# Low-rank products of a two-block model: row groups in turn, latents on more rows, two thin projections in one slab

## What is computed

```python
wl, al, gl = 64, 64 and 160 columns of ps
log_w = -softplus(-(w0 + tanh(wl) @ w_up)) - 0.5     # decay: rank 64
a = sigmoid(a0 + al @ a_up)                          # rate:  rank 64
g = sigmoid(gl) @ g_up                               # gate:  rank 160 = 128 + 32
if vl is not None:                                   # layer 1 only
    v = v + (v_first - v) * sigmoid(v0 + vl @ v_up)  # value: rank 32
...
y = group_norm(wkv7_scan(...)) * lnx_g + lnx_b
y = (y + bonus) * g
mixed = br_gate[0] * (y @ proj_a) + br_gate[1] * (pooled @ proj_b)
```

## Time and profile before

| | before |
|---|---|
| median of 3 runs | 2925.84 us (2925.13 to 2927.65) |
| profiled execution, first to last instruction (span) | 2918.1 us |
| TensorE matmul busy | 2791.1 us, 96% of the span |
| VectorE busy | 1587.6 us, 54% |
| ScalarE busy | 988.9 us, 34% |
| GpSimd busy | 200.0 us, 7% |
| mean granted TensorE clock | 0.976 of full speed |

### The profile page before, as it was taken

How to read it: one execution, slowest core, us unless ns; L and a number is a source line. 1 busy time by engine, 2 the same in 40 slices (tenths; PEclk the granted TensorE clock), 3 DMA queues, 4 the chain that set the end, 5 groups by cost and what they waited for, 6 DMA issues and landing times.

```text
span 2918.1 us, 46007 instructions
## 1 busy us (share of the span) xinstructions
PE 2791.1 (96%) x19577; PEld 2317.3 (79%) x19577; DVE 1587.6 (54%) x2309; ACT 988.9 (34%) x1354; POOL 200.0 (7%) x251
## 2 busy tenths in 40 slices
PE   8899999999999999998899999999988999999998
PEld 7778888897788888777878788887667778888887
DVE  5658777854677777465443553334575443543334
ACT  5643222335532212333333332223533333332223
POOL 4100000000000000010040000000020030000000
PEclk9999999999999999799999999999889999999999
DMA  4334555421145554210022322322220013223222
GB/s 150 101 104 131 180 165 173 156 64 53 52 130 177 176 168 152 66 58 12 3 77 89 99 90 98 101 97 72 72 64 6 24 52 101 95 93 101 95 93 72
DMA packets 238532, 281.98 MB, mean 97 GB/s; under 512 B 7444, under 2 KB 224856, under 8 KB 238344
## 3 DMA queue, kind: packets, MB, share of 16 engines
q1 hardware_dynamic: 225312, 227.07, 24.3%
q0 software_dynamic: 12896, 52.11, 6.0%
q10 hardware_dynamic: 136, 0.03, 0.0%
HBM read 277.09 MB, written 2.10 MB: 96 GB/s over the span
## 4 chain that ended last, share of the span: by engine, by line
PE 91%; DVE 4%; ACT 3%; issue 2%; DMA 0%; ACTq 0%; DVEq 0%; POOL 0%; POOLq 0%
PE psum L2386 25%; PE psum L2388 25%; PE psum L2387 25%; PE psum L2445 1%; PE psum L2446 1%; PE psum L2447 1%; PE psum L2887 1%; PE psum L2902 1%; DVE wlo L1522 1%; PE psum L2484 1%; PE psum L2870 1%; PE psum L2797 1%; ACT whi L848 1%; PE psum L2821 1%; PE psum L2835 1%
## 5 line engine op out<-in xcount | busy, mean ns | idle before, releaser
L2386 PE MATMUL psum<-hh,whi 128*128 128x512 f32 (+1 forms) x2040 | 794.4, 389 | 19.5 <-DVE hl L1562 6.6
L1522 DVE TENSOR_TENSOR wlo<-raw,whi 128x2048 fp32r<-128x2048 f32 x222 | 517.3, 2330 | 514.7 <-ACT whi L848 514.1
L2387 PE MATMUL psum<-hl,whi 128*128 128x512 f32 (+1 forms) x2040 | 787.6, 386 | 0.0
L2388 PE MATMUL psum<-hh,wlo 128*128 128x512 f32 (+1 forms) x2040 | 786.9, 386 | 0.0
L848 ACT ACTIVATE whi<-raw 128x2048 fp32r<-128x2048 f32 x222 | 423.8, 1909 | 550.7 <-PE psum L2388 550.7
L2386 PE MATMUL psum<-mh,whi 128*128 128x512 f32 (+1 forms) x1248 | 486.3, 390 | 3.1 <-issue 2.3
L2387 PE MATMUL psum<-ml,whi 128*128 128x512 f32 (+1 forms) x1248 | 480.1, 385 | 0.0
L2388 PE MATMUL psum<-mh,wlo 128*128 128x512 f32 (+1 forms) x1248 | 479.8, 384 | 0.0
L2386 PEld LDWEIGHTS psum<-hh,whi 128*128 128x128 f32 x2040 | 388.1, 190 | 104.0 <-issue 25.2
L2388 PEld LDWEIGHTS psum<-hh,wlo 128*128 128x128 f32 x2040 | 387.8, 190 | 76.9
L2387 PEld LDWEIGHTS psum<-hl,whi 128*128 128x128 f32 x2040 | 388.0, 190 | 75.9 <-issue 1.0
(11 more groups left out here) (451 smaller groups left out, 2848.0 us busy)
## 6 DMA issues: line engine op xcount, KB each, us to landing
rest<-in_ada_w POOLq DMA_DIRECT2D x64, 768.0 KB, 5.3
raw<-in_w_gu SPq DMA_DIRECT2D x44, 1024.0 KB, 5.1
raw<-in_w_in SPq DMA_DIRECT2D x34, 1024.0 KB, 5.2
raw<-in_w_mlp_in SPq DMA_DIRECT2D x32, 1024.0 KB, 5.4
raw<-in_w_mlp_out SPq DMA_DIRECT2D x32, 1024.0 KB, 5.1
raw<-in_w_out SPq DMA_DIRECT2D x16, 1024.0 KB, 5.1
raw<-in_w_down SPq DMA_DIRECT2D x16, 1024.0 KB, 5.1
raw<-in_w_mem_kv SPq DMA_DIRECT2D x8, 1024.0 KB, 5.2
```

What stands on the lines that cost most here:

```text
L1522: ins = dve.tensor_tensor(wlo[:, g % 2, :, :], raw[:, g % 2, :, :], f32(whi[:, g % 2, :, :]), ALU.subtract)
L2386: pe.matmul(out, whi_, xhi, start=first, stop=False)
L2387: pe.matmul(out, whi_, xlo, start=False, stop=False)
L2388: return pe.matmul(out, wlo_, xhi, start=False, stop=last)
```

## The change

- **Decay beside rate.** `lw` and `la` are issued in turn, tile by tile, instead of four and four.
- **Gate latents on more rows.** The 32 weight columns of `gl1` are copied side by side into the 128 columns of the slab while ScalarE and VectorE make `whi` and `wlo` (`latent_parts`, a broadcast read). The job so writes the 32 latents four times, on rows 0, 32, 64 and 96. In layer 0 each of the four gate tiles takes its own copy (`gate_rows`). The slab's load is 32 columns wide instead of 128.
- **Layer 1: both in one slab.** `v_down` is loaded beside the 32 gate columns, and the 64 columns are copied twice: gate latents on rows 0 and 64, value latents on rows 32 and 96 (`value_rows`). Slab and job `vl` are gone. `lv` takes rows 32 and 96 in turn, the gate's last 32 latents rows 0 and 64 in turn.
- **Gate order.** All four 128-row gate matmuls, then the four 32-row ones, then `gr`; no gate tile is left between `gr` and `g1`.
- **Loads.** `v_up` and the last 32 rows of `g_up` are loaded in four pieces each on GpSimd's queue (one before), and five more small rows of shift coefficients are loaded at the program's start on SyncE's queue.

```diff
+def gate_rows(l, t):
+    a = 64 * (t % 2) if l else 32 * t
+    return slice(a, a + 32)
+def value_rows(t):
+    a = 64 * (t % 2) + 32
+    return slice(a, a + 32)
...
             self.lin("gl1", l, 1, 1)
-            if l:
-                self.lin("vl", l, 1, 1)
             self.slab_jobs("k2", l, 0, 2)
...
+        def latent_parts(dst, src, g):
+            n = 64 if latents[g] else 32
+            x = src[:, g % 2, :, 0:n].rearrange("p k (a b) -> p k a b", a=1).to_broadcast([P, KT, P // n, n])
+            return dst[:, g % 2, :, 0:P].rearrange("p k (a b) -> p k a b", b=n), x
...
-                slab(plan.slab["gl1", l, 0], cols(w)[:, :, 14 * P:15 * P], n=P)
+                slab(plan.slab["gl1", l, 0], cols(w)[:, :, 14 * P:14 * P + 32], n=32)
                 if l:
-                    slab(plan.slab["vl", l, 0], cols(d["v_down_2"][0]), n=32)
+                    sp.dma_start(raw[:, plan.slab["gl1", l, 0] % 2, :, 32:64], cols(d["v_down_2"][0])).then_inc(s_vdown, 16)
...
-                act.activation(GL[0:32, 1, :], GL[0:32, 1, :], ACT.Sigmoid).then_inc(S("gate_latent"), 1)
+                for a in (slice(0, 32), slice(64, 96)) if l else (slice(0, P),):
+                    ins = act.activation(GL[a, 1, :], GL[a, 1, :], ACT.Sigmoid)
+                ins.then_inc(S("gate_latent"), 1)
...
                 for t in range(4):
                     p = start("lw", l, t)
                     done(pe.matmul(p, WA[0:HD, t * P:(t + 1) * P], LA[0:HD, :], start=True, stop=True))
-                for t in range(4):
                     p = start("la", l, t)
                     done(pe.matmul(p, WA[HD:P, t * P:(t + 1) * P], LA[HD:P, :], start=True, stop=True))
-                if l:
-                    evacuated(pe, J["vl", l, 0, 0])
-                    for t in range(4):
-                        p = start("lv", l, t)
-                        done(pe.matmul(p, VU[0:32, t * P:(t + 1) * P], VL[0:32, :], start=True, stop=True))
+                for t in range(4) if l else ():
+                    a = value_rows(t)
+                    p = start("lv", l, t)
+                    done(pe.matmul(p, VU[a, t * P:(t + 1) * P], GL[a, 1, :], start=True, stop=True))
...
-                gate(0)
-                gate(1)
+                p = [start("g", l, t) for t in range(4)]
+                for t in range(4):
+                    pe.matmul(p[t], GU[:, 0, t * P:(t + 1) * P], GL[:, 0, :], start=True, stop=False)
+                for t in range(4):
+                    a = gate_rows(l, t)
+                    done(pe.matmul(p[t], GU[a, 1, t * P:(t + 1) * P], GL[a, 1, :], start=False, stop=True))
                 pe.wait_ge(S("gn_inv"), l + 1)
                 for t in range(4):
                     done(head_factors(start("gr", l, t), t))
-                gate(2)
-                gate(3)
```

More of the change, by code:

```diff
@@ L579, in x_ready @@
                 evacuated(eng, J["fd", ((ver - 6) // 2, len(CHUNKS2) - 1), t // 2, t % 2])
+        latents = {plan.slab["gl1", l, 0]: l for l in range(2)}
+        def latent_parts(dst, src, g):
+            n = 64 if latents[g] else 32
+            x = src[:, g % 2, :, 0:n].rearrange("p k (a b) -> p k a b", a=1).to_broadcast([P, KT, P // n, n])
+            return dst[:, g % 2, :, 0:P].rearrange("p k (a b) -> p k a b", b=n), x
         def bc(m, n=4):
@@ L812, in _ @@
                 pool.dma_start(WA[HD:P, :], d["a_up_2"][l]).then_inc(s_lora, 16)
-                if l:
-                    pool.dma_start(VU[0:32, :], d["v_up_2"][0]).then_inc(s_lora, 16)
+                for t in range(4) if l else ():
+                    s = slice(t * P, (t + 1) * P)
+                    pool.dma_start(VU[value_rows(t), s], d["v_up_2"][0, :, s]).then_inc(s_lora, 16)
                 pool.wait_ge(S("decays"), 3 * l + 3)
@@ L826, in _ @@
                 pool.dma_start(GU[:, 0, :], d["g_up_2"][l, 0:P, :]).then_inc(s_lora, 16)
-                pool.dma_start(GU[0:32, 1, :], d["g_up_2"][l, P:P + 32, :]).then_inc(s_lora, 16)
+                for t in range(4):
+                    s = slice(t * P, (t + 1) * P)
+                    pool.dma_start(GU[gate_rows(l, t), 1, s], d["g_up_2"][l, P:P + 32, s]).then_inc(s_lora, 16)
                 pool.dma_start(PW, d["pool_w_2"][l].rearrange("g c d -> c g d")).then_inc(s_lora, 16)
@@ L1233, in _ @@
                 hi(plan.slab["gl1", l, 0] + 1)
[L1234 to L1237, removed]
+                own_part("gl1", 0, 0, c0 + 14, GL[:, 1, :])
                 evacuated(act, J["gl1", l, 0, 0])
@@ L1520, in lo @@
                     ins = dve.tensor_tensor(wlo_wide, raw_wide, f32(whi_wide), ALU.subtract)
+                elif g in latents:
+                    if latents[g]:
+                        dve.wait_ge(s_vdown, 16)
+                    low, x = latent_parts(wlo, raw, g)
+                    ins = dve.tensor_tensor(low, x, f32(latent_parts(whi, raw, g)[0]), ALU.subtract)
                 else:
@@ L2020, in _ @@
                 lo(plan.slab["gl1", l, 0] + 1)
[L2021 to L2024, removed]
+                before_part("gl1", 0, 0, V("mu_shift_2", m0 + 14), GL[:, 1, :])
                 for s in range(2):
@@ L2762, in _ @@
                 linear("gl1", l, 0, h, blocks=1)
[L2763 to L2764 removed]
                 linear("k2", l, 0, h)
[L2767 removed]
+                small = 128 * l + (32 if l == 0 else 96)
                 pe.wait_ge(s_lora, small)
@@ L3086, in _ @@
                 pe.wait_ge(S("gate_latent"), 2 * l + 2)
[L3087 to L3093, removed]
-                gate(0)
-                gate(1)
+                pe.wait_ge(s_lora, small + 96)
+                p = [start("g", l, t) for t in range(4)]
+                for t in range(4):
+                    pe.matmul(p[t], GU[:, 0, t * P:(t + 1) * P], GL[:, 0, :], start=True, stop=False)
+                for t in range(4):
+                    a = gate_rows(l, t)
+                    done(pe.matmul(p[t], GU[a, 1, t * P:(t + 1) * P], GL[a, 1, :], start=False, stop=True))
                 pe.wait_ge(S("gn_inv"), l + 1)
```

42 lines of the change are left out of this document (24 added, 18 removed), and 2 rows, old and new, of the table tiles.

## The result

The changed kernel takes **2957.32 us** (median of 4 runs, 2955.59 to 2961.43), beside 2925.49 for the kernel before in the same measurement: a ratio of 1.0108, with a 95% interval of 1.0094 to 1.0123. It is 1.1% slower; 2904 was forecast, and "slower" had a chance of 0.02.

A forecast was written before the change was run, and what follows sets the result against it. TensorE was taken as the bound, 91% of the chain that ended last; gains of 22.05 us off a 2918.1 us span gave 2896.05, plus 7.7 to the median, so 2904 us, range 2900.5 to 2912.5 with the low-clock rival.

The forecast's parts named there:

- 22.05 us off a span of 2918.1: Whole kernel: gains 1.7 + 5.44 + 4.75 + 1.66 + 5.1 + 3.4 us, leaving a span of 2896.05.
- Edits at no cost: Splits, larger sigmoid, start-up issues and extra GpSimd pieces: all hidden in slack; 0.6, 1.6 or about 0.5 us each if not.
- a pause at each alternation: Rival, chance 0.03: switching row groups costs 0.3 us each time instead of overlapping; loss of 5.6 us, time 2931.4.
- Low-rank stage, layer 0: `lw` and `la` alternated on two row groups take 3.75 us instead of 5.45: gain 1.7, bounds zero to 1.8.
- the assumed offset of 0.1: Layer 0's low-rank stage: the two row groups start 0.1 us apart; gain 1.8 if this vanishes.
- Layer 1: Low-rank stage: job `vl` gone, 5.44 us; `lw`, `la`, `lv` in 5.9 instead of 10.65, 4.75; full clock behind, 1.66.
- the clock's term: Layer 1's slab behind `lv`: full clock instead of half, gain 1.66 us, zero if the clock falls all the same.
- Gate stages: Layer 0 in 12.8 us instead of 17.95, gain 5.1; layer 1 in 13.5 instead of 16.93, gain 3.4.
- the wait that was forecast as 2.0 us: Before `g1`, both layers: TensorE waits 2.0 us for VectorE to free gate tile 0's bank, a new wait.
- That 5.6: Gate stages: eight 128-row instructions start at half clock, full clock returning midway; 5.6 us, bounds 5.0 and 6.9.
- The weighed estimate of 1.12 us: Layer 0's 32-row gate part on four row groups: 8 x 0.43 / 3.07 = 1.12 us, by the skill's speedup.
- The second rival: Chance 0.1: the clock falls in `gr` and the new wait, `g1` starts at half clock; 1.7 us per layer, time 2908.

The follow-up runs named there:

- after_pad112: The changed kernel with the filler tile `padding` back at 112 words instead of 113: 2906.18 us, ratio 0.9943 to the kernel before.
- gap256: The kernel before with 64 words put between `whi` and `wlo` and taken off the padding, moving `wlo` by 256 bytes: 2923.26 us, ratio 1.0007.
- both64: The kernel before with 16 filler words ahead of the slabs, so weights and activations all lie 64 bytes higher: 2924.17 us beside 2920.8.
- pad112_again: The changed kernel with `padding` at 112 words, measured a second time: 2903.29 us, ratio 0.9947 to the kernel before.
- gates_old: The changed kernel with padding at 112 and the gate order of the kernel before, keeping latents on more rows: 2913.15 us, ratio 0.9969.
- before_pad113: The kernel before with `padding` at 113 words instead of 112 and nothing else: 2971.72 us, ratio 1.0166.
- gap32: The kernel before with 8 words put between `whi` and `wlo` and taken off the padding, moving `wlo` by 32 bytes: 2972.84 us, ratio 1.0179.
- after_pad96: The changed kernel with `padding` at 96 words: 2955.34 us, ratio 1.0115 to the kernel before.
- before_pad48: The kernel before with a smaller padding, all activations 256 bytes lower: 2920.53 us beside a median of 2918.28.

## Why the prediction was wrong

**The step that failed** is the sum itself, "22.05 us off a span of 2918.1". It takes all that isn't listed as unchanged, and so sets the cost of the padding line to nothing; the part "Edits at no cost" doesn't name it. That line sets the pace of some 9,300 matmuls, and at 48.7 us it costs twice the sum of all gains. No rival had it: the one on the slow side was a pause at each alternation, and these pauses aren't there. With the pace restored the time was near the forecast, 2906.18 and 2903.29 for 2904. In part that is luck: the kernel before was faster in those two measurements as well (2923.03 and 2920.20, where the forecast started from 2925.84), and the gain was 16.9 us both times, not 22. The terms of the sum, against `after_pad112`:

**Low-rank stage, layer 0** (gain 1.7 predicted). The two row groups start within 0.01 us of each other, eight times:

```profile
1234.71 0.69 PE L2801 MATMUL psum<-rest 64*128 64x512 f32 x1
1234.72 0.69 PE L2803 MATMUL psum<-rest 64*128 64x512 f32 x1
1235.25 0.59 PE L2801 MATMUL psum<-rest 64*128 64x512 f32 x1
...
1238.35 0.50 PE L2417 MATMUL psum<-hh,whi 128*128 128x512 f32 x1
```

3.64 us for 5.45: gain 1.8, the assumed offset of 0.1 isn't there.

**Layer 1** (5.44 + 4.75 + 1.66). TensorE's order and ScalarE's evacuations there:

```profile
2077.37 0.69 PE L2801 MATMUL psum<-rest 64*128 64x512 f32 x1
...
2081.01 2.45 PE L2807 MATMUL psum<-rest 32*128 32x512 f32 x8
2083.38 0.50 PE L2417 MATMUL psum<-hh,whi 128*128 128x512 f32 x1
```

```profile
2066.60 0.69 ACT L1247 ACTIVATE rest<-psum,omm 128x512 f32<-128x512 f32 x1 [2.95 <-PE psum L2419]
...
2077.48 0.69 ACT L1247 ACTIVATE rest<-psum,omm 128x512 f32<-128x512 f32 x1 [2.62 <-PE psum L2419]
...
2089.16 0.69 ACT L1247 ACTIVATE rest<-psum,omm 128x512 f32<-128x512 f32 x1 [2.25 <-PE psum L2419]
```

`gl1` and the second job of `k2` stand 10.88 us apart, two jobs of 5.44: `vl` is gone and no wait has come for it. The small products take 6.01 us (5.9 predicted), and the slab behind them 5.78 to its first evacuation, where it took 7.48: the clock is full there, as forecast. Gains 5.44, 4.64 and 1.70.

The last two are too large as gains of the change, since they are taken from one trace of before, in which the clock happens to fall within `lv`. In two of the other three traces of that program at the same pace, `gap256` and `both64`, it doesn't, and the small products take 9.08 us instead of 10.65. `gap256`:

```profile
2089.90 2.41 PE L2772 MATMUL psum<-rest 64*128 64x512 f32 x5
...
2095.35 3.69 PE L2780 MATMUL psum<-rest 32*128 32x512 f32 x8
2098.98 0.50 PE L2386 MATMUL psum<-hh,whi 128*128 128x512 f32 x1
```

There the gain is 3.07, and a half-clock spell of the same 6.8 us comes later (2123.9 to 2130.7 for 2091.9 to 2098.8). From the first `lw` of layer 1 to its first gate product the four traces of before's program take 262.1 to 263.3 us, mean 262.7; the four of the changed one at that pace take 257.6 to 261.5, mean 259.8. So 2.9 us are won where 4.75 + 1.66 = 6.4 were forecast: the clock's term, and 1.6 us of the one before it, priced a spell whose place changes from one execution or copy to the next.

**Gate stages** (12.8 and 13.5 us predicted, 12.06 and 13.91 measured). Layer 1's, and the wait that was forecast as 2.0 us:

```profile
2337.11 6.12 PE L3117 MATMUL psum<-rest 128*128 128x512 f32 x8
2343.16 1.99 PE L3120 MATMUL psum<-rest 32*128 32x512 f32 x8
2345.08 3.71 PE L2824 MATMUL psum<-ident,hn 128*64 128x128 f32 x64
2351.02 0.47 PE L2417 MATMUL psum<-hh,whi 128*128 128x512 f32 x1 [2.23 <-DVE rest L2273]
```

It is 1.97 us in layer 0 and 2.23 here, released by VectorE's multiplication by `g`. The eight full-row instructions took 5.31 and 6.05 us against 5.6 forecast, the small ones 1.07 on four row groups (1.1) and 1.92 on two (1.8). That 5.6 was met is in part luck as well: the forecast has them begin at half clock, but in layer 0 the clock was full when they began and fell later, and in layer 0 of `pad112_again` and in both layers of the changed kernel's own trace all eight ran at full clock, in 3.61 us. The wait ahead of `g1` was 3.12, 2.85 and 2.10 us there. The weighed estimate of 1.12 us for the four-group part rests on the 3.07 times that the Trainium skill gives (TensorE: Matmul & The Clock Gate, Measured speedup vs the span model); the 1.07 here, 8 x 0.43 / 1.07 = 3.2 times, agrees with it.

**The second rival** (chance 0.1: the clock falls once more at `gr` and the wait) came true in part, beside the forecast: in layer 1 the clock is at its half from 2352 to 2356, which costs 1.7 us; in layer 0 of this trace it stays full. In `pad112_again` and in the changed kernel's own trace it falls in both layers.

**What is missing.** The measured terms are 1.8 + 5.4 + 4.6 + 1.7 + 5.9 + 3.0 = 22.4, less the 1.7: 20.7. The times give 16.9 in both measurements (by the intervals 0.36 to 0.78% of 2923, 11 to 23 us, and 0.39 to 0.68%, 11 to 20). `gates_old` says on which side the rest lies: the gates are worth the 8.9 of their rows and more, while the low-rank terms sum to 13.6 in the rows and to 7.1 in the times, at most 12.6. Of the 6.5 us between, 6.3 - 2.9 = 3.4 are the stretch of layer 1 above. Part of them shows in the scan of layer 1, which lies in that stretch, where TensorE's idle that nothing in the profile explains sums to 5.3 to 5.7 us in three traces of the kernel before and its shifted copies, and to 7.0 to 8.0 in five of changed kernels. The largest in before and in `after_pad112`:

```profile
PE psum L2887 <- issue: 1.3, 3, 0.6
...
PE psum L2952 <- issue: 1.1, 1, 1.1
```

```profile
PE psum L2929 <- issue: 2.7, 2, 1.5
...
PE psum L2987 <- issue: 1.6, 1, 1.6
```

Line 2929 is line 2902 of before, and neither is in the diff. That is some 2 us given back; why, no run here settles. The other 3 us of the 6.5 stay open as well; the intervals are wide enough to hold most of them. Single executions also differ by up to 6 us before layer 0's low-rank stage begins (`lw` at 1228.73 in before, at 1234.6 in `gap256`), which is why the medians decide and not the spans.

## What to carry to other kernels

Read the diff for what it does to the addresses of tensors that it doesn't mention: one that grows by four bytes can move all behind it by 32, and here this outweighed every gain. After such a change compare first the start-to-start distance of an untouched, common matmul, far away from the edit; if that has moved, the cause is global, and local traces won't find it. And an interleaving that leaves TensorE waiting for another engine can be improved by moving independent work into that wait, at no cost in work.

## What the runs showed of the hardware

- In this stream of 128x512 fp32r matmuls, each with a weight load of its own, the pace at full clock goes with the distance between the activations and the weights in SBUF: 226.8 ns where it is a multiple of 256 bytes, 229.0 at 64 over, 232.5 at 128, 233.3 at 32, -32 and -64. Shifting both together changes nothing (`both64`). At half clock the starts stand 0.427 us apart in before and 0.426 in `before_pad113`: there the distance costs nothing. One of the two weight slabs shifted by 32 bytes is enough for 233.3 on average (`gap32`), with 238.8 ns for the step in which that slab's weights are loaded, 228.5 and 232.5 for the others. The mechanism isn't shown; `gap32` speaks against one in which a matmul pays only for its own weights, or only for those loaded while it streams.
- Two groups of 64 rows, addressed in turn, start within 0.01 us of each other, a pair every 0.43 us; four groups of 32 rows took 1.07 us for eight instructions that take 0.43 each.
- The wait of TensorE ahead of `g1` was followed by a half-clock spell of some 3.4 us in six of eight cases: the changed kernel itself (waits of 2.85 and 2.10 us), `pad112_again` (3.12 and 2.23), and layer 1 of `after_pad112` (2.23) and of `after_pad96` (2.20). It was not in layer 0 of the last two, behind 1.97 and 2.80 us. So the length of the wait alone doesn't tell.
- A half-clock spell can come at another place in the same program: that of 6.8 us which falls in `lv` in the traces of before and `before_pad48` comes some 27 us further on in `gap256` and `both64`, counted from the first `lw`.
